# Rows of the experts fetched by indirect transfers, where a matrix product picked them

## What is computed

```python
expert = (grp[:, None] * EXPERTS_PER_GROUP + top_idx).reshape(-1)
...
def expert_block(args):
    tok, e, w = args
    xb = h_pad[tok]
    y = (jax.nn.silu(xb @ w_gate[e]) * (xb @ w_up[e])) @ w_down[e]
    return y * w[:, None]
```

## Time and profile before

| | before |
|---|---|
| time, median of 3 runs | 1119.99 us (1116.12 to 1122.78) |
| the profiled execution's own time | 1115.26 us |
| its span | 1113.4 us |
| TensorE busy | 1063.6 us, 96% |
| VectorE, ScalarE, GpSimd busy | 271.6, 233.2, 98.9 us |
| moved by DMA | 286.32 MB |
| mean granted TensorE clock | 0.98 |

### The profile page before, as it was taken

The page is one execution under the profiler, slowest core; times in us unless marked ns, Lnnn a source line. Parts: engine busy times, 40 slices in busy tenths (PEclk is TensorE's granted clock), DMA queues, the critical chain, the costliest instruction groups (busy, mean ns, idle before and its releaser), DMA issues.

```text
span 1113.4 us, 14021 instructions
## 1 busy us (share of the span) xinstructions
PE 1063.6 (96%) x5662; PEld 550.4 (49%) x5662; DVE 271.6 (24%) x729; ACT 233.2 (21%) x488; POOL 98.9 (9%) x142
## 2 busy tenths in 40 slices
PE   6999999999999999999969999999999999999994
PEld 3468877555666667775543333333333333333442
DVE  1122011465433424111241111111111111121413
ACT  2012001166322244000211111111111111111334
POOL 0020031000223220000020000000000000001000
PEclk9999999999999999999969999999999999999997
DMA  9962239220545578563328999999999999999801
GB/s 329 265 214 56 76 75 191 76 76 1 162 130 162 183 283 196 210 227 151 137 90 327 419 422 422 423 424 425 423 422 423 424 424 423 422 421 423 280 1 49
DMA packets 65443, 286.32 MB, mean 257 GB/s; under 512 B 10273, under 2 KB 14650, under 8 KB 44844
## 3 DMA queue, kind: packets, MB, share of 16 engines
q1 hardware_dynamic: 55068, 256.67, 59.8%
q0 software_dynamic: 9936, 28.46, 8.9%
q10 hardware_dynamic: 384, 0.41, 0.1%
HBM read 276.57 MB, written 18.25 MB: 265 GB/s over the span
## 4 chain that ended last, share of the span: by engine, by line
PE 50%; DMA 10%; issue 1%; DVE 1%; ACT 0%; SPq 0%; POOL 0%; POOLq 0%; DVEq 0%
PE ps L1060 17%; DMA ring<-in_w_exp_up_dram 10%; PE ps L556 9%; PE ps L1084 7%; PE ps L1037 6%; PE ps L612 5%; PE ps L1045 1%; PE ps L577 1%; PE ps L1074 1%; PE ps L984 1%; PE ps L619 1%; PE ps L593 1%; PE ps L840 0%; PE ps L547 0%; PE ps L1026 0%
## 5 line engine op out<-in xcount | busy, mean ns | idle before, releaser
L1060 PE MATMUL ps<-ring,reg_xh 128*64 128x512 f32 x512 | 150.4, 602 | 5.0 <-DMA ring<-in_w_exp_up_dram 3.3
L1060 PE MATMUL ps<-late,reg_xh 128*64 128x512 f32 x336 | 148.6, 595 | 2.1 <-DMA reg_k<-in_w_exp_up_dram 1.3
L1037 PE MATMUL ps<-reg_xh 128*64 128x512 f32 x384 | 90.6, 607 | 1.7 <-DVE reg_xh L1882 1.7
L1060 PEld LDWEIGHTS ps<-ring,reg_xh 128*64 128x64 f32 x512 | 47.2, 138 | 89.8 <-issue 88.2
L1407 ACT ACTIVATE reg_xh<-ps 64x512 f32<-64x512 f32 x32 | 34.2, 1068 | 227.8 <-PE ps L1060 227.8
L1946 DVE TENSOR_TENSOR reg_xh<-reg_xh,ps 64x512 f32<-64x512 f32 x32 | 22.1, 691 | 240.5 <-ACT reg_xh L1407 240.5
L1060 PE MATMUL ps<-reg_k,reg_xh 128*64 128x512 f32 x176 | 77.9, 595 | 0.0
L826 PE MATMUL ps<-reg_xh,ring 128*128 128x320 f32 x256 | 73.5, 436 | 0.0
L1060 PEld LDWEIGHTS ps<-late,reg_xh 128*64 128x64 f32 x336 | 44.3, 137 | 46.2 <-issue 44.7
L2151 POOL DMA_INDIRECT y_rows<-reg_xh,slot_row x29 | 28.3, 975 | 395.2 <-ACT reg_xh L1418 354.6
L720 PE MATMUL ps<-reg_xh,ring 128*128 128x285 f32 (+1 forms) x256 | 60.1, 397 | 2.0 <-ACT reg_xh L1258 2.0
(11 more groups left out here) (377 smaller groups left out, 1281.9 us busy)
## 6 DMA issues: line engine op xcount, KB each, us to landing
ring<-in_w_exp_gate_dram SPq DMA_DIRECT2D x21, 2048.0 KB, 21.1
ring<-in_w_in_dram SPq DMA_DIRECT2D x13, 2048.0 KB, 11.1
late<-in_w_exp_gate_dram SPq DMA_DIRECT2D x11, 2048.0 KB, 20.1
reg_k<-in_w_exp_up_dram SPq DMA_DIRECT2D x11, 2048.0 KB, 24.6
ring<-in_w_exp_down_dram SPq DMA_DIRECT2D x11, 2048.0 KB, 24.5
ring<-in_w_exp_up_dram SPq DMA_DIRECT2D x11, 2048.0 KB, 25.6
reg_o<-in_w_exp_down_dram SPq DMA_DIRECT2D x11, 2048.0 KB, 25.7
late<-in_w_exp_up_dram SPq DMA_DIRECT2D x10, 2048.0 KB, 25.1
```

Source lines behind the costliest of these rows:

```text
L1037: last = pe.matmul(out[64 * c:64 * c + 64, :], bufs[:, t, :], xn2[:, t, 512 * c:512 * c + 512], start=(t == 0), stop=(t == 2))
L1060: last = pe.matmul(out[64 * part:64 * part + 64, :], xb[:, k, :], ws_[part][:, k, :], start=(k == 0), stop=(k == KT - 1))
```

## The change

The rows of the experts 0 to 3 are picked by products as before. From expert 4 on (`SUMMED` is 4) they are fetched from memory. Ahead of the loop GpSimd writes the normalised rows twice to a new scratch tensor `xn_rows` of 640 rows, in four direct transfers, since the table counts a row's first choice from 0 and its second from 320 on. In the loop GpSimd issues, behind the store of expert e, an indirect transfer that reads the half rows of expert e+4 by the same table into `xg`, of which there are now two; it waits for `xg_turned` first, that is until the buffer's rows of expert e+2 were turned. TensorE's `turn_rows` waits for the transfer (`fetched`). From expert 4 on, `gather` on TensorE, `select` on VectorE and the copy on ScalarE are gone. The second `xg` buffer is a part of `reg_k` that no weight buffer uses.

```diff
 EXPERT_SLOTS = ((5, 6, 0), (1, 2, 7), (3, 4, 8))
+SUMMED = 4
 STORED = NE - 3
...
         ye = [reg_x[:, a:a + 512] for a in (7168, 4096)]
-        xg = reg_x[:, 3072:3584]
+        xg = [reg_x[:, 3072:3584], reg_k[:, 4096:4608]]
         sel = [reg_x[:, 3584 + 192 * i:3776 + 192 * i].rearrange("p (t n) -> p t n", t=3) for i in range(2)]
...
         row_of = scratch("row_of", (SLOTS * NE, 1))
+        xn_rows = scratch("xn_rows", (2 * N, D))
         y_more = scratch("y_more", (NE * MORE, D))
...
         gain_e_in = sem("gain_e_in")
+        fetched, xn_out = [sem(f"fetched{i}") for i in range(2)], sem("xn_out")
         blank, blanked, row_put, row_in = sem("blank"), sem("blanked"), sem("row_put"), sem("row_in")
...
-            def turn_rows(s_ready, count, s_done, bank=7):
+            def turn_rows(s_ready, count, rows, s_done, bank=7):
...
                 for m in range(4):
-                    last = pe.transpose(ps[:, bank, 128 * m:128 * m + 128], xg[:, 128 * m:128 * m + 128], ident)
+                    last = pe.transpose(ps[:, bank, 128 * m:128 * m + 128], rows[:, 128 * m:128 * m + 128], ident)
                 last.then_inc(s_done, 1)
...
             gather(sel[0], ps[:, 0, :], sel_ready, 1, gathered)
-            turn_rows(xg_ready, 1, xg_turned)
+            turn_rows(xg_ready, 1, xg[0], xg_turned)
...
                 gate_up(slots[w_gate], slots[w_up], xe[par], ps[:, 2 + par, :]).then_inc(up_done, 1)
-                if not last_one:
+                by_sums = keep in (-1, -2) and p + 1 < SUMMED
+                if by_sums:
                     gather(sel[1 - par], ps[:, 1 - par, :], sel_ready, e + 2, gathered)
...
                     down(slots[w_down], he[1 - par], ps[:, 5 - par, :], (0, 1))
-                if not last_one:
-                    turn_rows(xg_ready, e + 2, xg_turned)
+                if by_sums:
+                    turn_rows(xg_ready, e + 2, xg[1 - par], xg_turned)
+                elif not last_one:
+                    turn_rows(fetched[1 - par], (i * 3 + (p + 1 - SUMMED) // 2 + 1) * 16, xg[1 - par], xg_turned)
                 if first:
...
             for p in range(6):
-                expert(0, p, -1 if p == 0 else None)
+                expert(0, p, -1 if p == 0 else -2)
             with pe.Fori(1, 4) as i:
...
-            def activated(i, par, last_one=False):
+            def activated(i, par, by_sums=False):
...
                 act.activation(sg.rearrange("p (m q) -> p q m", m=4), ps[0:64, 2 + par, :].rearrange("p (q m) -> p q m", m=4), ACT.Silu).then_inc(silu_done, 1)
-                if not last_one:
+                if by_sums:
...
                     act.wait_ge(gathered, e + 2)
-                    act.activation(xg, ps[:, 1 - par, :], ACT.Copy).then_inc(xg_ready, 1)
+                    act.activation(xg[1 - par], ps[:, 1 - par, :], ACT.Copy).then_inc(xg_ready, 1)
...
             act.wait_ge(gathered, 1)
-            act.activation(xg, ps[:, 0, :], ACT.Copy).then_inc(xg_ready, 1)
-            activated(0, 0)
-            activated(0, 1)
+            act.activation(xg[0], ps[:, 0, :], ACT.Copy).then_inc(xg_ready, 1)
+            activated(0, 0, True)
+            activated(0, 1, True)
             result(0, 0, True)
-            activated(1, 0)
+            activated(1, 0, True)
             result(0, 1, True)
...
             result(NE // 2 - 2, 1)
-            activated(NE // 2 - 1, 1, True)
+            activated(NE // 2 - 1, 1)
             result(NE // 2 - 1, 0)
...
-            def expert_steps(i, par, last_one=False, keep=None, first=False):
+            def expert_steps(i, par, last_one=False, keep=None, first=False, by_sums=False):
                 e = i * 2 + par
...
                     weigh_slots(keep)
-                if not last_one and keep != 2:
+                if by_sums:
                     dve.wait_ge(gathered, e + 1)
...
             times_gain(xe[0]).then_inc(xe_ready, 1)
-            expert_steps(0, 0, first=True)
-            expert_steps(0, 1)
+            expert_steps(0, 0, first=True, by_sums=True)
+            expert_steps(0, 1, by_sums=True)
             with dve.Fori(1, NE // 2 - 2) as i:
...
             half_rows = y_rows.rearrange("r (c n) -> (r c) n", c=2)
+            xn_half_rows = xn_rows.rearrange("r (c n) -> (r c) n", c=2)
             more_rows = y_more.rearrange("(e r) n -> e r n", e=NE)
...
+            pool.wait_ge(xn_dve, 2)
+            pool.wait_ge(xn_act, 1)
+            for k in range(2):
+                pool.dma_start(xn_rows[N * k:N * k + NP, :].rearrange("(t p) n -> p t n", p=128), xn2[:, 0:2, :]).then_inc(xn_out, 16)
+                pool.dma_start(xn_rows[N * k + NP:N * k + N, :], xn2[0:64, 2, :]).then_inc(xn_out, 16)
             pool.wait_ge(blanked, 96)
...
                                         bounds_check=4 * N - 1, oob_is_err=False).then_inc(ye_out[e % 2], 16)
+                if e == 0:
+                    pool.wait_ge(xn_out, 64)
+                if e + SUMMED < NE:
+                    pool.wait_ge(xg_turned, e + SUMMED - 1)
+                    pool.indirect_dma_start(xg[e % 2], None, xn_half_rows, bass.IndirectOffsetOnAxis(ap=target[:, e + SUMMED:e + SUMMED + 1], axis=0),
+                                            bounds_check=4 * N - 1, oob_is_err=False).then_inc(fetched[e % 2], 16)
             pool.wait_ge(ye_out[0], (STORED // 2 + 1) * 16)
```

More of the change, by code:

```diff
@@ L1176, in _ @@
                         pe.wait_ge(ov["ye"], n)
-                        turn_rows(ov["xg"], n, ov["xg_turned"], 5)
+                        turn_rows(ov["xg"], n, xg[0], ov["xg_turned"], 5)
                         if blk == 0:
@@ L1450, in _ @@
                         act.wait_ge(ov["gathered"], n)
-                        act.activation(xg, ps[:, 4, :], ACT.Copy).then_inc(ov["xg"], 1)
+                        act.activation(xg[0], ps[:, 4, :], ACT.Copy).then_inc(ov["xg"], 1)
                         act.wait_ge(ov["up"], n)
```

## The result

The changed kernel takes 1129.98 us (median of 5 runs, 1128.08 to 1134.74), the kernel before 1119.79 us (5 runs, 1115.95 to 1122.78). The ratio is 1.011 with a 95% interval of 1.0086 to 1.0133: slower, by some 10 to 15 us. Forecast were 1129.5 us and a loss of 10 us.

A forecast was written before the change was run, and what follows sets the result against it. The weight stream was taken as the bound. Removal 0, table 0, fetches 9.0, reads 0.5 and clock 0.5 made 10 us more on a median of 1119.99: 1129.5 us rounded, range 1119.5 to 1137.

The forecast's parts named there:

- The bound: Stage of 32 experts: the weight stream allows one expert each 15.15 us, while TensorE could do one in 14.17 us.
- The removal: Expert loop: 28 selection products, 72 us of TensorE, leave; waits for weights grow equally, so the gain is nothing.
- The table of rows: Ahead of the loop: four writes, 2.6 MB, fall where DMA is nearly idle; cost nothing, 6 us if they ran past it.
- The fetches: Behind the first 28 stores: each costs the slowest DMA engine 0.32 us, 9.0 us in all; bounds nothing and 12 us.
- The even share: Fetches spread evenly over engines: 0.22 us each, 6.3 us for 28; chance 0.09 for 5.6 to 8 us more, 0.04 for 4 to 5.6.
- The reads of the stored rows: Beside the last up matrix: expert 28's earlier end lets GpSimd's six reads take more of its landing, 0.5 us.
- The clock: Last gate and up: a longer wait ahead lowers the granted clock; up to another 1.7 us lost, 0.5 taken.
- rival B: Expert loop: TensorE's waits lower its clock, costing only where an expert loses over 3.9 us; 1135 to 1140 us, chance 0.05.
- The waits that were added: Expert loop: GpSimd's wait for `xg_turned` and TensorE's for `fetched` cost nothing.
- The sum: Whole kernel: 0 + 0 + 9.0 + 0.5 + 0.5 = 10 us more, median forecast 1129.5 us.
- A: Fetches in the loop miss the engine that stores delay, so they hide; 1120 to 1121 us, chance 0.12.
- C: Expert loop: TensorE was the bound in most executions, so the removal pays 5 to 8 us at most; 1112 to 1115 us, chance 0.04.

The follow-up runs named there:

- products and fetches together: Kernel before, keeping all selection products, plus the table of rows and 28 fetches into a buffer nobody reads: 1131.3 us, ratio 1.0119.
- crowded places: Changed kernel with ranks placed to fill one DMA engine's eight places before the next engine's, same bytes: 1150.46 us, ratio 1.0295.
- late reads: GpSimd's six reads of stored rows wait for the last up matrix: on the kernel before 1119.79 us, ratio 1.0007; with places spread over engines too, 1113.46 us.
- removal alone: Changed kernel without the table's writes, the fetches and the wait for them, later experts on stale rows: 1119.32 us, ratio 1.0011 to the kernel before.
- empty fetches: Changed kernel with all fetched places but row 0 left out, the 28 transfers still issued and waited for: 1122.35 us, ratio 1.0049.
- two rearranged kernels: Changed kernel with only places dealt out otherwise: spread over the DMA engines 1127.15 us, filling one engine before the next 1150.46 us.

## Why the prediction was right, step by step

- *The bound.* Right. Removing 72 us of TensorE's work alone changed nothing (1.0011), and the pace stayed at 15.16 us.
- *The removal: nothing.* Right, by the same run, and from the other side by products and fetches together (1.0119 against 1.011).
- *The table of rows: nothing.* Right (0.9986), though the writes didn't all lie in idle time: from 566 to 570 us the DMA share is 1.04 in the changed kernel, where it was 0.15, and from 570 to 572 us 0.96 for 0.00. Nothing waited for that.
- *The fetches: 0.32 us each on the slowest engine, 9.0 us.* The mechanism was right, and crowded places showed it: 20 us more with the same bytes. The size was too low. The pace went from 15.15 to 15.54 us, so a fetch costs 0.39 us, 10.9 us in all. I had taken the price of a store. The runs split the 0.39: 0.08 for the transfer with nothing in it (15.24 against 15.16), 0.30 for the rows (15.54 against 15.24). The 10.9 us are inside the bounds of 0 and 12. That a fetch costs more than a store isn't shown. In the traces a packet with two filled places (4,096 bytes) takes 161 ns in the changed kernel, where about half of these transfers are fetches, and 160 ns in the kernel before, where all are stores; one with two empty places (8 bytes) takes 10 ns. A transfer has 80 packets, five to an engine if they are dealt evenly. So four filled places on an engine make two full packets, two empty ones and the last small one, an estimate of 0.35 us for a store and a fetch alike; an empty transfer makes 0.05 us. The 0.32 was read from the landing of one matrix.
- *The even share, 0.22 us.* The fetches' even share is 0.26 us, 7.4 us for 28, and the loss inside the loop is 10.9: the even share is too low a price, as the prediction had it.
- *The reads of the stored rows: 0.5 us.* The last interval is 2.35 us over the pace (17.89 - 15.54) where it was 1.76: 0.6 us. The late reads confirm that they are what makes it long, and that taking them away has its own price. That the 0.6 comes of TensorE's earlier end isn't shown: with the reads of the stored rows as early as before this excess is 1.1 to 1.8 us in the four profiles with products and 1.4 to 2.6 us in four without, 4.4 with crowded places.
- *The clock: 0.5 us on the last product.* It is 1.1 us (9.87 against 8.78) between two profiles. It scatters: with the reads as early as before it took 8.48 to 9.87 us in the five kernels without products, after waits of 3.9 to 6.7 us, and 7.09 to 8.79 us in the four with them, after 1.8 to 2.1 us. So the direction is borne out and the size isn't. Inside the loop rival B's sum held. The clock didn't fall in each expert: of the 22 gate-and-up products from 693.88 to 1021.52 us ten took 7.09 us, the others 8.5 to 8.8. The removal alone has the same mixture after waits of 1.3 to 3.6 us, and still 15.16 us an expert.
- *The waits that were added: nothing.* Right. The fetches land in 8.3 us, and no idle time of TensorE ends in one.
- *The sum.* 10.9 + 0.6 + 1.1 = 12.6 us from the profile, against 12.0 + 1.1 = 13.1 measured there; 10.0 forecast; 10.2 between the medians, and 9.6 to 14.9 us by the interval of the ratio. So the forecast of 1129.5 fits the median better than its terms deserve: they were some 2.5 us short together, and the medians lie at the low end of what the ratio allows. That much of the fit is luck. The last gate and up was to start near 1034 us with 89 us behind it; it started at 1039.41 us, with 92.2 behind it.
- *Rivals.* A (hidden fetches) fell with the products and fetches together, C (TensorE was the bound) with the removal alone; so did B as a cause of the loss, since the waits and the low clock are there without it. Even shares alone fell with crowded places.

One thing is open. Three kernels in which TensorE follows the landings have one interval some 1.3 us longer than the rest near 740 us: 16.87 us in the changed kernel, from 724.90 to 741.77 us, and 16.3 and 16.5 with the removal alone and with empty fetches. The three with rearranged places and without the products don't have it. In the kernel before the weights were ahead of TensorE then, so it would not be seen. What it is was not tried.

## What to carry to other kernels

When the weights' stream sets the pace, work on the engine that waits for it is free, and a transfer that replaces it is not. Price an added transfer by what it puts on the busiest DMA engine, not by its bytes over the bandwidth: an indirect transfer that leaves places out can, as the crowded places bear out, put all of its rows on a few engines. Dealing the used places out evenly costs one small copy and gained 0.4% here.

## What the runs showed of the hardware

- Bytes that stay the same and are dealt out otherwise made 1127, 1130 and 1150 us. Four and four partitions to an engine, as the Trainium skill ("DMA: Bandwidth & Descriptors", The descriptor swizzle) has it for a direct transfer, gave the pace of the two rearranged kernels ahead of their runs to within 0.05 us an expert (15.36 expected, 15.39 measured; 16.2 and 16.19).
- An indirect transfer whose places were all left out, but for row 0's, still cost 0.08 us on the path, and raised the queue's share from 1.6% to 2.0%.
- In that transfer's queue (q0) a packet with two filled places took 160 to 161 ns, in stores and fetches alike, and one with two empty places 10 ns.
- SyncE's issue of a load takes 0.37 us at the start of the stage and up to 5.6 us in the rows shown of the kernel before once the weights set the pace; the longest there is 6.34 us, at 976.23 us. I had not looked for saturation in the issuing engine.
